# Partial sums, a third tile in each entry, and three additions on GpSimd in a kernel of two transformer blocks

## The reference, cut to what matters

```python
def second_block(x, ...):
    h = x
    for i in range(2):
        g = norm_gains[i]
        f = swiglu(rmsnorm(h, g[0]), ffn_gate[i, 0], ffn_up[i, 0], ffn_down[i, 0])      # 1024 -> 2816 -> 1024
        h = h + 0.5 * rmsnorm(f, g[1])
        mix = hybrid_mixer(rmsnorm(h, g[2]), ...)                                       # two kinds of attention
        h = h + rmsnorm(mix, g[3])
        f = swiglu(rmsnorm(h, g[4]), ffn_gate[i, 1], ffn_up[i, 1], ffn_down[i, 1])
        h = h + 0.5 * rmsnorm(f, g[5])
        gate = sigmoid(rmsnorm(h, g[6]) @ w_ple_gate[i])
        h = h + rmsnorm((p[i] @ w_ple[i]) * gate, g[7])
    return h

def rmsnorm(x, g):
    return x * rsqrt(mean(x * x, axis=-1) + 1e-6) * g
```

## Time and profile before

| | |
|---|---|
| median of 3 runs | 3004.84 us (3004.49 to 3005.7) |
| the profiled execution's own time | 3005.28 us |
| its span, first to last instruction | 3003.5 us |
| share of the span: PE, DVE, ACT, POOL | 95%, 52%, 38%, 8% |
| mean granted clock of PE | 0.98 |

### The profile page before, as it was taken

One profiled execution on the slowest core, in us unless ns is written; L12 is line 12 of the kernel. 1 busy time (PEld: TensorE's weight loads), 2 busy tenths in 40 slices (PEclk: granted clock), 3 DMA queues, 4 the chain that ended last, 5 costly groups with the idle time before them and its releaser, 6 DMA issues.

```text
span 3003.5 us, 42576 instructions
## 1 busy us (share of the span) xinstructions
PE 2862.1 (95%) x17236; PEld 2384.8 (79%) x17236; DVE 1558.5 (52%) x2618; ACT 1145.5 (38%) x1861; POOL 243.3 (8%) x272
## 2 busy tenths in 40 slices
PE   6999889899999999999999999899999999999997
PEld 3866888778788888777888888788888778888886
DVE  5744465544354434855644436644436755644346
ACT  3333444243333323455433224532324564333234
POOL 0000065400000000200000000000000201000000
PEclk7999999999999999999999999999999999999998
DMA  6222000022232332301222332233332301332321
GB/s 237 64 67 73 3 8 3 15 91 92 77 106 98 98 106 92 117 32 50 72 97 98 99 106 78 77 98 99 98 105 96 95 29 43 98 98 93 104 91 57
DMA packets 69778, 244.92 MB, mean 82 GB/s; under 512 B 8464, under 2 KB 10640, under 8 KB 68944
## 3 DMA queue, kind: packets, MB, share of 16 engines
q1 hardware_dynamic: 69584, 242.21, 24.5%
HBM read 234.70 MB, written 3.15 MB: 79 GB/s over the span
## 4 chain that ended last, share of the span: by engine, by line
PE 67%; DVE 3%; ACT 2%; issue 1%; DVEq 0%; ACTq 0%
PE pair L228 20%; PE pair L230 20%; PE pair L229 20%; PE pair L2568 2%; PE pair L2597 2%; PE pair L357 2%; PE pair L2607 1%; ACT w_hi_at L182 1%; DVE rstd_at L473 1%; DVE work_at L308 0%; DVE w_lo_at L190 0%; PE pair L491 0%; DVE residual L314 0%; DVE h_lo_at L319 0%; PE pair L488 0%
## 5 line engine op out<-in xcount | busy, mean ns | idle before, releaser
L228 PE MATMUL pair<-h_hi_at,w_hi_at 128*128 128x512 f32 (+1 forms) x2048 | 781.3, 381 | 35.9 <-DVE h_lo_at L319 31.4
L229 PE MATMUL pair<-h_lo_at,w_hi_at 128*128 128x512 f32 (+1 forms) x2048 | 759.1, 371 | 0.0
L230 PE MATMUL pair<-h_hi_at,w_lo_at 128*128 128x512 f32 (+1 forms) x2048 | 759.0, 371 | 0.0
L190 DVE TENSOR_TENSOR w_lo_at<-w_raw,w_hi_at 128x1024 fp32r<-128x1024 f32 x348 | 439.4, 1263 | 430.6 <-ACT w_hi_at L182 430.4
L182 ACT ACTIVATE w_hi_at<-w_raw 128x1024 fp32r<-128x1024 f32 x348 | 364.8, 1052 | 523.5 <-PE pair L230 512.1
L228 PEld LDWEIGHTS pair<-h_hi_at,w_hi_at 128*128 128x128 f32 x2048 | 389.0, 190 | 112.2 <-DVE h_lo_at L319 37.4
L229 PEld LDWEIGHTS pair<-h_lo_at,w_hi_at 128*128 128x128 f32 x2048 | 389.1, 190 | 67.1 <-issue 0.5
L230 PEld LDWEIGHTS pair<-h_hi_at,w_lo_at 128*128 128x128 f32 x2048 | 388.9, 190 | 65.3
L2330 DVE TENSOR_TENSOR work_at<-pair,rstd_at 128x512 f32<-128x512 f32 (+1 forms) x184 | 122.1, 667 | 363.2 <-PE pair L230 363.1
L228 PE MATMUL pair<-a_hi_at,w_hi_at 128*128 128x512 f32 (+1 forms) x792 | 290.1, 366 | 0.0
L229 PE MATMUL pair<-a_lo_at,w_hi_at 128*128 128x512 f32 (+1 forms) x792 | 289.4, 365 | 0.0
(11 more groups left out here) (423 smaller groups left out, 3975.8 us busy)
## 6 DMA issues: line engine op xcount, KB each, us to landing
w_raw<-in_weights SPq DMA_DIRECT2D x431, 512.0 KB, 3.4
residual<-in_x SPq DMA_DIRECT2D x1, 2048.0 KB, 12.0
cos_sin_at<-rope_table SPq DMA_DIRECT2D x2, 1024.0 KB, 4.8
by_sin_at<-delta_at SPq DMA_DIRECT2D x32, 64.0 KB, 2.0
by_sin_at<-kd_at SPq DMA_DIRECT2D x32, 64.0 KB, 2.0
out<-residual SPq DMA_DIRECT2D x16, 128.0 KB, 1.7
q_wide<-in_ctx SPq DMA_DIRECT2D x1, 1024.0 KB, 12.9
rope_table<-zb SPq DMA_DIRECT2D x1, 1024.0 KB, 4.2
```

What stands on the lines that cost most here:

```text
L190: eng.tensor_tensor(self.w_lo[:, g % self.split].rearrange("p k n -> p (k n)"), self.w_raw[:, g % RAW], self.w_hi[:, g % self.split].rearr ...
L228: pe.matmul(out, sh, mh, start=start, stop=False)
L229: pe.matmul(out, sh, ml, start=False, stop=False)
L230: return pe.matmul(out, sl, mh, start=False, stop=stop)
```

## The change

1. **Sums by column groups.** The 16 matmuls (128 ones columns by 256) of an entry become four batches. A batch is four matmuls that have 32 columns of ones and four tiles of squares, each writing 32 partitions of the bank, after n = 3, 7, 11 and 15. ACT copies the result (`act_partial`) and a single matmul with the ones adds the four groups (`pe_fold`). Each group holds its sum 32 times over, hence the 1/(32·D). The fold of half 0 stands behind n = 11, that of half 1 in the tile after the entry.
2. **Three tiles in the entry.** The third output tile's triples are made in the entry as well, one step behind the first two. In `Ple` its first half goes with n = 8 to 15 and its second half stands behind the last batch.
3. **Order.** The third granule's remainder is made at step 3 instead of 8, the fourth's at step 8. The squares of a tile come behind the next tile's rounding. The squares, the sum and the root of the exit's half 1 move ahead by one or two steps. The reciprocals of the two halves have a `w_make_lo` between them. All drains are one instruction of 512 columns. `w_make_hi`/`w_make_lo` in the loops stand behind drains, for one granule later. Other banks are used in turn. In `Mixer` the sum of the exit's half 0 moves from the last tile's third triple to the next-to-last tile's fourth.
4. **Last.** GpSimd makes three of the last half's additions.
5. **Window attention.** Score matmuls take the keys of two blocks at once where two are left: 80 matmuls of up to 256 columns instead of 144 of 128.

The diff, cut to its core:

```diff
 class Entry:
-    FIRST_BANKS = ((0, 1), (6, 7))
+    FIRST_BANKS = (0, 1, 7)
+    BEHIND = 1
...
+    def pe_sums(self, pe, batch):
+        half, second = divmod(batch, 2)
+        pe.wait_ge(*self.squared(4 * batch + 4))
+        for q in range(4):
+            last = pe.matmul(self.kit.banks[self.SUM_BANK[half]][32 * q:32 * q + 32, 0:HALF], self.kit.square("ones")[:, 0:32],
+                             self.sq[:, q], start=not second, stop=bool(second), skip_group_check=True)
+        last.then_inc(self.summed.sem, 1)
+
+    def pe_fold(self, pe, half):
+        pe.wait_ge(*self.part_copied(half + 1))
+        pe.matmul(self.kit.banks[self.SUM_BANK[half]][:, HALF:], self.kit.square("ones"), self.partial[:, cols(half)],
+                  start=True, stop=True).then_inc(self.folded.sem, 1)
...
     def pe(self, pe):
-        for half in range(2):
-            for t in range(KD):
-                self.pe_products(pe, half, t)
-                if self.leave and half == 0 and t == 1:
-                    self.leave.pe_sum(pe, 1)
-                if t >= 1:
-                    self.pe_sum(pe, half, t - 1)
-            self.pe_sum(pe, half, KD - 1)
+        for n in range(2 * KD):
+            if n in (4, 8, 12):
+                self.pe_sums(pe, n // 4 - 1)
+            for m in range(2):
+                self.pe_product(pe, n, m)
+            if self.leave and n == self.leave.LATE_SUM:
+                self.leave.pe_sum(pe, 1)
+            if n >= self.BEHIND:
+                self.pe_product(pe, n - self.BEHIND, 2)
+            if n == 11:
+                self.pe_fold(pe, 0)
+        self.pe_sums(pe, 3)
+        for n in range(2 * KD - self.BEHIND, 2 * KD):
+            self.pe_product(pe, n, 2)
...
-        makes = {KD: lambda: kit.w_make_lo(dve, self.g0 + 2)}
+        makes = {3: lambda: kit.w_make_lo(dve, self.g0 + 2), KD: lambda: kit.w_make_lo(dve, self.g0 + 3)}
...
 class Exit:
+    LATE_SQUARES, LATE_ROOT, LATE_SUM = 1, 3, 0
...
 class Last:
+    POOL_TILES = (2, 4, 6)
...
     def pool(self, pool):
-        pass
+        x, c = self.kit.residual, cols(1)
+        for t in self.POOL_TILES:
+            pool.wait_ge(*self.scaled(KD + t + 1))
+            pool.tensor_tensor(x[:, t, c], x[:, t, c], self.buf[:, t], ALU.add).then_inc(self.pool_added.sem, 1)
...
-                if t >= 1:
+                if t >= 1 and not (half and t - 1 in self.POOL_TILES):
                     add(t - 1)
...
 class Ffn:
         for f in range(FT):
-            kit.w_make_hi(act, g0 + 2 * f + 3)
+            kit.w_make_hi(act, g0 + 2 * f + 4)
+            if f == 0:
+                self.entry.act_root(act, 1)
...
             act.activation(self.gate[:, f % 2], self.gate[:, f % 2], ACT.Silu).then_inc(self.gate_silu.sem, 1)
-            kit.w_make_hi(act, g0 + 2 * f + 4)
+            if f < FT - 1:
+                kit.w_make_hi(act, g0 + 2 * f + 5)
...
 class Mixer:
-                    if half == 1 and t == KD - 1 and k == 1:
+                    if half == 1 and t == KD - 2 and k == 2:
                         self.exit.pe_sum(pe, 0)
```

More of the change, by code:

```diff
@@ L372, in first_parts @@
[L372 to L386 removed]
+            act.wait_ge(*self.summed(n // 4))
@@ L506, in __init__, with there @@
         self.buf = kit.work.rearrange("p a (b n) -> p (a b) n", b=2)
-        self.scaled, self.added = kit.mark("scaled", 2 * KD), kit.mark("added", 2 * KD)
+        self.scaled, self.added = kit.mark("scaled", 2 * KD), kit.mark("added", 2 * KD - len(self.POOL_TILES))
+        self.pool_added = kit.mark("pool_added", len(self.POOL_TILES))
         self.stored = kit.mark("stored", 32 * KD)
+    def there(self, half, t):
+        before = sum(p < t for p in self.POOL_TILES) if half else 0
+        return self.pool_added(before + 1) if half and t in self.POOL_TILES else self.added(half * KD + t - before + 1)
     def sp(self, sp):
@@ L2502, in pe @@
         self.entry.pe(pe)
-        for t in range(2, self.TILES):
-            if t == 3:
+        for t in range(3, self.TILES):
+            if t == 4:
                 pe.wait_ge(*self.entry.rooted(2))
-            if t >= 4:
-                pe.wait_ge(*self.drained(t - 3 if t < 6 else max(t - 5, 2)))
+            if t >= 5 and t != 7:
+                pe.wait_ge(*self.drained(max(i for i in range(t) if self.RING[i] == self.RING[t]) + 1))
             if t == 4:
@@ L2840, in dve @@
                    b["kd"][:, t - 8])
-            for bank, c in self.entry.first_parts(t) if t < 2 else [(self.bank(t), slice(0, SEQ))]:
-                last = dve.tensor_tensor(dst[:, c], bank, kit.rstd[:, c], ALU.mult)
-            last.then_inc(self.drained.sem, 1)
+            dve.tensor_tensor(dst, self.bank(t), kit.rstd[:, :], ALU.mult).then_inc(self.drained.sem, 1)
+            if 0 < t < self.TILES - 1:
+                kit.w_make_lo(dve, g0 + t + 4)
         for r in (6, 7):
```

267 lines of the change are left out of this document (152 added, 115 removed).

## The result

The changed kernel takes 2975.19 us (median of 4 runs, 2970.63 to 2978.31), the kernel before in the same comparison 3005.27 (3004.49 to 3005.97). The ratio is 0.9899 with a 95% interval of 0.9882 to 0.9916: 30 us or 1.0% faster. The forecast was 2964, with a range of 2951 to 2983. The new runs are spread over 7.7 us, those of before over 1.5; but 21 later runs of the kernel before lay between 3002.11 and 3010.33, 8.2 us apart, so the wider spread is no mark of the changed kernel. The profiled execution is the slowest of the four, 2978.31 with a span of 2976.5.

The account below looks back on a forecast made before the run. PE's own work was taken to bound the kernel, busy 2862 of 3003.5 us. Entries and exits −39.5, window −2.5, Last +1.2 make −40.8 from 3005.3: 2964 us, range 2951 to 2983, the forecast's own 2957 to 2971.

Parts of the forecast that it names:

- The price of a batch: In each entry, four sums made at once cost PE 0.66 us, with bounds of 0.43 and 1.95.
- Rival 2: In the entries, batches don't overlap: each takes 1.95 us, 41 us in all, so 3005, no change; chance 0.04.
- The path in the second Ffn's entry: DVE's 13.1 us to the remainder of n = 8, then PE's 11.0: third tile ends at 24.1, where it was 29.5.
- The exit's sum: At the Mixer's exit, half 0's sum stands seven triples (2.5 us) earlier; PE's wait falls from 3.31 to 0.9.
- The second part of the path: In the second Ffn's entry, PE from n = 8 on: 8 steps, three batches and a fold, 11.0 us.
- Ple's entry: PE's work falls by 3.1 us net and 1.4 of 1.8 idle vanishes, filled by third-tile triples: 4.5 gained.
- The wait before the next layer's first Ffn: At Ple's exit, PE's 5.85 us wait for the first remainder falls by 1.15, part of 2.4 gained there.
- Rival 1: In entries, ACT's rounding and DVE's remainder wait for each other; only the sums' work is won: 2979; chance 0.20.
- Window scores: In window attention, merged score matmuls save 2.5 us, with bounds of nothing and 6.4.
- the end: In Last, GpSimd's three additions hold DVE still: they cost 2.2 us and save 1.0, so 1.2 slower.
- Order at no cost: Behind entries, moved granules, roots and drains cost nothing, hidden by PE's work on the next two tiles.
- rival 3: In Ffn's loop, a granule comes late and PE may wait in each of 84 steps: 3059 us; chance 0.03.

Follow-up runs that it names:

- the turned queue: The changed kernel with ACT's squares of n = 4, 8 and 12 queued behind the rounding of n + 2 instead of ahead: 2976.84 us, ratio 0.9903 to the kernel before.

## Why the prediction was right, and where it wasn't

**Right in kind and place.** The forecast was faster, by shorter entries, and the gain is in the entries. The price of a batch, the term with the widest bounds, was 0.66 and measured 0.66 by the same reading, 0.76 with the slower triple behind it. Rival 2 (no overlap) would need 1.95. The path in the second Ffn's entry is there to 0.1: from the remainder of n = 0 to that of n = 8 I had 13.1, and the trace has 13.06 (1443.38 to 1456.44). The exit's sum moved 2.5 us out of PE's wait (3.31 to 0.79; forecast 0.9).

**The second part of the path, mis-sized by 0.7 an entry.** I had 11.0 from the remainder of n = 8 to the third tile's end. In the second Ffn it was 24.81 − 13.1 = 11.7. One triple was left out: the third tile is one step behind, so that at n = 8 its n = 7 is still to do, 0.36. And a batch with the triple behind it costs 0.76, not 0.66, three times: 0.3. Together that is the 0.7. The same holds for Mixer (25.30 against 24.6); in the next layer's first Ffn it was 0.3 (27.49 against 27.2). Five entries make about 3 of the missing 8 us. In the first Ffn it was more, 24.33 against 23.0: 0.53 is the wait that the turned queue on ACT took away, 0.4 are the four batches, and the last 0.4 stays open; its slow start (granted clock 0.88) was there before as well (0.89).

**Ple's entry, the step that failed.** "Of its 1.8 us of idle time I take 1.4 to vanish, since the third tile's triples fill it": they can't, since they stand behind the products that wait. The wait stayed, 1.60 and 0.29, but what ended its longer part was now ACT's drain and no longer the granule. The second Ple gained 2.2 in place of 4.5. The first gained 5.15 of 5.75, and that was luck: 1.25 is the wait at its exit that vanished as forecast, 2.2 is what the second gained, and the rest goes with the lower clock of the kernel before (0.96 in that entry). The experiment won 1.54 back with an earlier drain.

**The waits that stayed.** The wait before the next layer's first Ffn fell from 5.85 to 5.42, by 0.43 where 1.15 was forecast; its cause was not looked into. PE still waits 25.1 us for the remainder, where the prediction had about 13: beside this 5.42 there are 5.11 before the first Ffn, as in the kernel before, and 7.7 in the eight waits of about 1 us for the inverse and the fourth granule in the entries of the Mixers and second Ffns.

**Rival 1 in small.** The coupling that it names is there: ACT waited 47.7 us for batches. But with the third tile inside it costs nothing but the 0.53 in the first Ffn, as the turned queue shows.

**Window scores and the end.** 2.5 was forecast for the scores, with bounds of 0 and 6.4; the stage shows some 0.5, which can't be told from 0. For the end I had 1.2 slower and it is 0.4: the exclusion is right, but a GpSimd addition, 0.84 long here, held DVE for 0.46 and not for 0.73. The Trainium skill ("SBUF — State Buffer", "Who interferes with whom") calls the port pair that the two share an exclusive lock. The rows agree with it in kind, by the 0.46, but that is about half of the addition's recorded length. How the two shared the rest they don't show.

**Order at no cost**: held. No wait of PE for a granule appeared in the loops, and rival 3 had no row.

**The rest.** The stages gained some 33 us, the medians 30; the difference I put down to episodes, as far as the profiled execution shows them. The median then lies 11 us above the forecast, and the forecast's own range (2957 to 2971) is missed; the stated one holds it.

## What to carry to other kernels

A path written out instruction by instruction was right to 0.1 us where one engine sets the pace, and off by 0.7 where the pace passes to another: ask what that engine has left undone at the point where it takes over, and price an inserted batch up to the end of the triple behind it. Idle time that stands ahead of an engine's first instruction can't be filled with work that is queued behind it. Two parts that both shorten one stretch needn't share a gain; undo each with the other in place and with it gone, and look at what is left with both gone: here it was slower than the kernel before.

## What was not expected of the hardware

Executions of one program differ by episodes of the lower clock at places where the code is the same: 28 matmuls in 6.08 us in one profile and 3.24 in the thirteen others. Stages outside of such episodes repeat to 0.02 us over different kernels (369.67, 369.68, 369.69 for a second Ffn), which makes a stage of one profile a finer measure than the median of four totals. It is so only where the granted clock is looked at too: the first Mixer took 265.5 in some profiles and 267.1 in others, with the same code.
